# First experts of a PEER layer selected between the splits of the query projection, and ten row buffers for the first token tile

## The reference

```
h2 = rms_norm(x, norm2_g)
q = (h2 @ wq).reshape(T, 8, 2, 128)
scores = einsum('thcd,hcnd->thcn', q, keys)
s_top, i_top = top_k(scores, 16)
cand = s_top[:, :, 0, :, None] + s_top[:, :, 1, None, :]
cand_idx = i_top[:, :, 0, :, None] * 128 + i_top[:, :, 1, None, :]
best, pos = top_k(cand.reshape(T, 8, 256), 16)
idx = take_along_axis(cand_idx.reshape(T, 8, 256), pos, axis=-1)
gate = softmax(best)
hid = gelu(einsum('td,thkd->thk', h2, U[idx]))
x = x + einsum('thk,thkd->td', gate * hid, Vt[idx])
out = rms_norm(x, norm_f_g)
```

## Time and profile before

| | |
|---|---|
| median of 3 runs | 2193.09 us (2183.55 to 2193.47) |
| profiled execution | 2183.11 us, of which span 2181.4 us |
| busy: PE, DVE, ACT, POOL | 1477.1, 1641.9, 837.4, 975.7 us |
| splits (L798), 136 | 314.7 us, 2315 ns each |
| dots (L1331) read from `acc`, 189 | 428.3 us, 2284 ns each |
| gathers of U (L450), 256 | 250.5 us of GpSimd, 979 ns each |
| GpSimd products (L458), 63 | 285.6 us, 4533 ns each |

### The profile page before, as it was taken

One profiled execution on the slowest core, in us unless ns is written; L12 is line 12 of the kernel. 1 busy time (PEld: TensorE's weight loads), 2 busy tenths in 40 slices (PEclk: granted clock), 3 DMA queues, 4 the chain that ended last, 5 costly groups with the idle time before them and its releaser, 6 DMA issues.

```text
span 2181.4 us, 26401 instructions
## 1 busy us (share of the span) xinstructions
PE 1477.1 (68%) x9809; PEld 1368.3 (63%) x9809; DVE 1641.9 (75%) x2172; ACT 837.4 (38%) x1008; POOL 975.7 (45%) x692
## 2 busy tenths in 40 slices
PE   6999999999999999700000000113358999999996
PEld 6987998899999889700000000113247999899996
DVE  5465774545654555798898899998878999999997
ACT  4353433333433444112121221446666444444443
POOL 1002220000000000188888878877747776667763
PEclk9999999999999999855555555555569999999998
DMA  5555443434455554399999999999905999999996
GB/s 194 173 175 191 137 153 126 155 136 158 171 174 175 194 192 168 144 422 421 418 415 414 416 386 404 419 404 369 359 26 191 357 359 354 346 369 356 360 357 224
DMA packets 151526, 597.80 MB, mean 274 GB/s; under 512 B 14688, under 2 KB 14704, under 8 KB 118000
## 3 DMA queue, kind: packets, MB, share of 16 engines
q0 software_dynamic: 58048, 356.02, 41.3%
q1 hardware_dynamic: 93360, 240.22, 31.2%
HBM read 594.09 MB, written 2.10 MB: 273 GB/s over the span
## 4 chain that ended last, share of the span: by engine, by line
PE 47%; issue 15%; DVE 14%; DMA 11%; POOL 8%; ACT 4%; DVEq 0%; POOLq 0%; SPq 0%; ACTq 0%
PE acc L1470 9%; PE acc L1473 8%; PE acc L1472 8%; DMA slots<-in_peer_u,expert 8%; DVE slots L1331 7%; POOL starts L487 6%; DMA starts<-in_v_gather,expert 3%; PE acc L1487 3%; PE acc L1489 3%; PE acc L1488 3%; PE scr L1740 3%; POOL slots L450 1%; PE scr L1535 1%; PE acc L1770 1%; PE acc L1772 1%
## 5 line engine op out<-in xcount | busy, mean ns | idle before, releaser
L798 DVE TENSOR_TENSOR w_lo<-raw,w_hi 128x2048 fp32r<-128x2048 f32 x136 | 314.7, 2315 | 319.5 <-ACT w_hi L503 318.5
L1331 DVE SCALAR_TENSOR_TENSOR slots<-slots,acc 128x2048 f32<-128x2048 f32 x189 | 428.3, 2284 | 36.4 <-DMA slots<-in_peer_u,expert 34.6
L503 ACT ACTIVATE w_hi<-raw 128x2048 fp32r<-128x2048 f32 x136 | 260.1, 1913 | 435.6 <-PE acc L1473 308.0
L487 POOL DMA_INDIRECT starts<-in_v_gather,expert x256 | 344.5, 1346 | 155.4 <-DVE X L1411 103.8
L450 POOL DMA_INDIRECT slots<-in_peer_u,expert x256 | 250.5, 979 | 288.8 <-DVE expert L1267 188.4
L458 POOL TENSOR_TENSOR slots<-slots,N 128x2048 f32<-128x2048 f32 x63 | 285.6, 4533 | 31.6 <-DMA slots<-in_peer_u,expert 31.2
L1470 PE MATMUL acc<-hT_hi,w_hi 128*128 128x256 f32 x1024 | 294.6, 288 | 3.1 <-PE acc L1473 2.5
L1472 PE MATMUL acc<-hT_lo,w_hi 128*128 128x256 f32 x1024 | 292.2, 285 | 0.0
L1473 PE MATMUL acc<-hT_hi,w_lo 128*128 128x256 f32 x1024 | 292.1, 285 | 0.0
L1740 PE MATMUL scr<-hot_a,hot_b 128*128 128x128 f32 x512 | 101.4, 364 | 280.5 <-ACT hot_a L732 171.9
L771 ACT ACTIVATE v_hi<-v_raw 128x1408 fp32r<-128x1408 f32 x128 | 177.0, 1384 | 282.3 <-PE scr L1772 203.6
(11 more groups left out here) (262 smaller groups left out, 3324.1 us busy)
## 6 DMA issues: line engine op xcount, KB each, us to landing
raw<-in_w_in SPq DMA_DIRECT2D x88, 1024.0 KB, 4.8
v_raw<-in_v_dense SPq DMA_DIRECT2D x128, 704.0 KB, 6.4
raw<-in_w_o SPq DMA_DIRECT2D x16, 1024.0 KB, 5.1
raw<-in_peer_wq SPq DMA_DIRECT2D x16, 1024.0 KB, 5.0
raw<-in_w_a_up SPq DMA_DIRECT2D x8, 1024.0 KB, 5.1
raw<-in_w_b_up SPq DMA_DIRECT2D x8, 1024.0 KB, 5.0
slots<-in_peer_u,expert POOLq DMA_INDIRECT x256, 9.0
starts<-in_v_gather,expert POOLq DMA_INDIRECT x256, 6.6
```

Of the source, the lines that this page charges most:

```text
L487: pool.indirect_dma_start(starts[s % CRING][:, :], None, v_gather[:, :], bass.IndirectOffsetOnAxis(ap=expert[:, s // NSEL, s % NSEL:s % NS ...
L503: a.activation(w_hi[:, m % 2, :, :], raw[:, m % 2, :, :], ACT.Copy).then_inc(hi_ready, 1)
L798: v.tensor_tensor(w_lo[:, m % 2, :, :], raw[:, m % 2, :, :], w_hi[:, m % 2, :, :].bitcast(fp32), ALU.subtract).then_inc(lo_ready, 1)
L1331: v.scalar_tensor_tensor(out=slots[:, j, :], in0=slots[:, j, :], scalar=1.0, in1=row, op0=ALU.mult, op1=ALU.mult, accum_out=hid[:, t, k:k + 1]
```

## The change

`slots` becomes ten buffers, placed one by one (`ROW_AT`, in KB): the first two at 24 and 152 KB, where the projection has nothing, then the eight of before. Rows 0 to 3 use buffers 0 to 3, which all lie outside the projection's buffers; so do rows 4 to 7, after rows 0 to 3 are used. From row 4 to row 123 the ten go round, from row 124 on the last eight. Gather 0 now waits for `group_done` = `G_WQ` and gather 8, in place of gather 2, for `G_END`. On VectorE all eight parts of pair 0 and the dots of rows 0 to 3 stand between the splits of groups 1 to 3; row 3 is a VectorE row now, so there are 62 GpSimd products. Score 0 stands behind the first unit of group 1 on PE instead of the second. The sums move from `hid` to the room of `fox_mask`, since `hid` shares its room with `h2T_hi`, which the projection still reads.

```diff
+ROW_AT = (24, 152, 32, 40, 48, 56, 64, 72, 80, 88)
+LAST_TEN = 124
...
 def on_pool(q):
-    return q % FOUR == FOUR - 1 and q != GATHERS - 1
+    return q % FOUR == FOUR - 1 and FOUR <= q < GATHERS - 1
+
+def buffer_of(q):
+    if q < FOUR:
+        return q
+    if q < LAST_TEN:
+        return (q - FOUR) % len(ROW_AT)
+    return 2 + (q - LAST_TEN) % SLOTS
...
-        slots = at("slots", 32, [SLOTS, D])
+        slots = [at(f"slots{j}", kib, [D]) for j, kib in enumerate(ROW_AT)]
...
+        hid_sum = fox_mask[:, :].rearrange("p (t k) -> p t k", t=NT)
...
-                if q == 2:
+                if q == 0:
+                    pool.wait_ge(group_done, G_WQ)
+                if q == 2 * FOUR:
                     pool.wait_ge(group_done, G_END)
-                if q >= SLOTS:
-                    pool.wait_ge(row_used[j], q // SLOTS)
+                if uses_before(q, j):
+                    pool.wait_ge(row_used[j], uses_before(q, j))
...
-                if n:
+                if on_pool(FOUR * n - 1):
                     product(FOUR * n - 1)
...
-            for n in range(1, 4):
-                lo(G_WQ + n, 0)
-                lo(G_WQ + n, 1)
-                copy_q(n - 1)
-                lo(G_WQ + n, 2)
-                copy_scores(n - 1)
-                if n < 3:
-                    top_keys(0, 2 * n - 2)
-                lo(G_WQ + n, 3)
-                if n < 3:
-                    top_keys(0, 2 * n - 1)
-                else:
-                    for part in range(4, 8):
-                        select_part(0, 0, part)
+            lo(G_WQ + 1, 0)
+            copy_q(0)
+            lo(G_WQ + 1, 1)
+            copy_scores(0)
+            select_part(0, 0, 0)
+            lo(G_WQ + 1, 2)
+            select_part(0, 0, 1)
+            select_part(0, 0, 2)
+            lo(G_WQ + 1, 3)
+            select_part(0, 0, 3)
+            select_part(0, 0, 4)
+            lo(G_WQ + 2, 0)
+            select_part(0, 0, 5)
+            lo(G_WQ + 2, 1)
+            copy_q(1)
+            select_part(0, 0, 6)
+            lo(G_WQ + 2, 2)
+            select_part(0, 0, 7)
+            copy_scores(1)
+            lo(G_WQ + 2, 3)
+            dve.wait_ge(h2_ready, NT)
+            lo(G_WQ + 3, 0)
+            dot(0)
+            lo(G_WQ + 3, 1)
+            copy_q(2)
+            dot(1)
+            lo(G_WQ + 3, 2)
+            copy_scores(2)
+            dot(2)
+            lo(G_WQ + 3, 3)
+            dot(3)
             copy_q(3)
...
-                    if not on_pool(q):
+                    if q >= FOUR and not on_pool(q):
                         dot(q)
...
-                    if n and m == 1:
+                    if n and m == (n > 1):
                         score(n - 1)
```

More of the change, by code:

```diff
@@ L97, in on_pool, with uses_before @@
 def on_pool(q):
-    return q % FOUR == FOUR - 1 and q != GATHERS - 1
+    return q % FOUR == FOUR - 1 and FOUR <= q < GATHERS - 1
[5 more added lines that the diff above has]
+    return 2 + (q - LAST_TEN) % SLOTS
+def uses_before(q, j):
+    return sum(buffer_of(p) == j for p in range(q))
 def spread(g):
@@ L304, in build @@
         granted, granted_w = sem("granted"), sem("granted_w")
-        row_landed = [sem(f"row_landed{j}") for j in range(SLOTS)]
-        row_used = [sem(f"row_used{j}") for j in range(SLOTS)]
+        row_landed = [sem(f"row_landed{j}") for j in range(len(ROW_AT))]
+        row_used = [sem(f"row_used{j}") for j in range(len(ROW_AT))]
         h2_rows, product_ready = sem("h2_rows"), sem("product_ready")
@@ L694, in sum_product @@
             def sum_product(q):
-                act.wait_ge(product_ready, q // FOUR + 1)
-                row = slots[:, q % SLOTS, :]
-                a.activation(row, row, ACT.Copy, accum_out=hid[:, q // NSEL, q % NSEL:q % NSEL + 1]
-                             ).then_inc(row_used[q % SLOTS], 1)
+                act.wait_ge(product_ready, sum(map(on_pool, range(q + 1))))
+                row = slots[buffer_of(q)][:, :]
+                a.activation(row, row, ACT.Copy, accum_out=hid_sum[:, q // NSEL, q % NSEL:q % NSEL + 1]
+                             ).then_inc(row_used[buffer_of(q)], 1)
             def weight_curves(t):
@@ L737, in _ @@
                     rows_to_psum(1)
-                if i < GROUPS - 1:
+                if on_pool(FOUR * i + FOUR - 1):
                     sum_product(FOUR * i + FOUR - 1)
@@ L1285, in copy_scores, with dot @@
                 dve.sem_inc(scr_free[half], 1)
[L1287 to L1300 removed]
+            def dot(q):
+                t, k, j = q // NSEL, q % NSEL, buffer_of(q)
+                row = N1[:, t, :]
+                if q >= FOUR and k >= 2:
+                    dve.wait_ge(h2_rows, 2 * t + 2)
+                    row = acc[:, :, :].rearrange("p a n -> p (a n)")
+                dve.wait_ge(row_landed[j], 16 * (uses_before(q, j) + 1))
+                v.scalar_tensor_tensor(out=slots[j][:, :], in0=slots[j][:, :], scalar=1.0, in1=row,
+                                       op0=ALU.mult, op1=ALU.mult, accum_out=hid_sum[:, t, k:k + 1]
+                                       ).then_inc(row_used[j], 1)
+            lo(G_WQ + 1, 0)
[29 more added lines that the diff above has]
+            dot(3)
             copy_q(3)
@@ L1321, in hot_first @@
                                 ALU.is_equal).then_inc(a_ready[2], 1)
-            def dot(q):
-                t, k, j = q // NSEL, q % NSEL, q % SLOTS
-                row = N1[:, t, :]
-                if k >= 2:
-                    dve.wait_ge(h2_rows, 2 * t + 2)
-                    row = acc[:, :, :].rearrange("p a n -> p (a n)")
-                dve.wait_ge(row_landed[j], 16 * (q // SLOTS + 1))
-                v.scalar_tensor_tensor(out=slots[:, j, :], in0=slots[:, j, :], scalar=1.0, in1=row,
-                                       op0=ALU.mult, op1=ALU.mult, accum_out=hid[:, t, k:k + 1]
-                                       ).then_inc(row_used[j], 1)
             def weights(t):
-                for j in range(SLOTS):
-                    dve.wait_ge(row_used[j], (t + 1) * NSEL // SLOTS)
+                for j in range(len(ROW_AT)):
+                    dve.wait_ge(row_used[j], uses_before((t + 1) * NSEL, j))
                 g3 = gate[:, :].rearrange("p (h k) -> p h k", h=H)
```

23 lines of the change are left out of this document (11 added, 12 removed).

## The result

| us | before | after |
|---|---|---|
| median | 2192.07 (6 runs, 2183.55 to 2194.54) | 2172.43 (6 runs, 2163.77 to 2174.65) |
| profiled execution, its span | 2183.11, 2181.4 | 2163.77, 2162.1 |
| projection's last product begins | 909.10 | 913.81 |
| first gather; first gather behind the projection | 913.67, the same one | 874.65 (row 0); 914.99 (row 8) |
| gather of row 36 | 1002.50 | 984.54 |

The ratio is 0.9917 (95%: 0.99 to 0.9934), 0.83% faster. The forecast was 2172.0 us. The profiled executions lie at the low end of the runs on both sides and are 19.3 us apart.

What follows compares the result with a forecast made beforehand. The row stream (DMA) was taken as the limit from 920 to 1240 us, with later work following the rows. 19.9 + 2.6 - 0.9 = 21.6 us off the median 2193.09 gave 2171.5, predicted as 2172; range 2159 to 2175, whole range up to 2184.

Steps and rivals of the forecast that it cites:

- The rows that leave the stream: Gathers 0 to 7 move into the projection; eight rows of 2.485 us each gain 19.9 us.
- the hold of 0.9: After the seam, gathers wait for VectorE to free buffers; gather 16 lands 0.9 us late, once; bounds 0 to 3 us.
- The seam: From projection to row stream: gather 8 begins at 911.1 instead of 913.67, a gain of 2.6 us.
- the raw loads: Projection's loads beside the four early gathers: no delay to PE, taken as 0, at most some 5 us.
- (a): Group 1, unit 2 of the projection: the split ends 0.3 us after PE could have begun.
- (b): Group 2, unit 0 of the projection: parts 3 and 4 delay the next split, PE begins 0.9 us late.
- (c): Group 3, unit 3 of the projection: scores 2 and dot 2 come first, PE begins 0.8 us late.
- the two old waits: PE's two waits for late splits in the kernel before, 0.3 us each, were to go, saving 0.6 us.
- the second rival: A raw load waits behind the four early gathers, PE stalls 5 us or more; gain 16, 2177 us; chance 0.07.
- The rival that VectorE sets the pace: Behind the seam only VectorE's 9.4 us lead counts, 2184 us; chance 0.13, shared with the lead lost after 1240 us.
- PE's clock: Rival: a new wait in the projection halves PE's clock for eight units, costing 46 us; 2217 us, chance 0.05.
- It does what it says: Rival it doesn't: rows 4 to 7 are held, only four rows leave the stream; 2181 us, chance 0.05.

Runs made afterwards that it cites:

- Four rows early: Changed kernel with gather 4 instead of gather 8 waiting for the projection's end, so four rows leave the stream; 2182.13 us, ratio 0.996.
- none early: Changed kernel with all gathers and dots 0 to 3 behind the projection, early selection and ten buffers kept; 2186.54 us, ratio 0.9991.
- order: Changed kernel with VectorE's splits and selection parts in the projection reordered so that no split comes late; 2173.26 us, ratio 0.9924.
- both: Changed kernel with VectorE's reordered splits and selection and the early gathers queued one at a time; 2166.37 us, ratio 0.9891.
- after again: The changed kernel, unaltered, measured and traced a second time; 2173.65 us, ratio 0.9918.
- Paced: Changed kernel with gathers 1, 2 and 3 each waiting for one more split of group 3; 2168.79 us, ratio 0.9896.
- work added at row 64: Changed kernel with three unused VectorE maxima, 5.3 us in all, before the dots of group i = 16; 2168.78 us, ratio 0.9905.
- eight buffers: Changed kernel with a ring of eight buffers instead of ten from row 8 on; 2182.53 us, ratio 0.9966.
- work added at the seam: Changed kernel with three unused VectorE maxima, 5.3 us in all, behind the last copy_q; 2176.28 us, ratio 0.9943.
- held product: Changed kernel with GpSimd's product of row 139 waiting until the weights of tile 0 are ready; 2170.89 us, ratio 0.9909.
- both and held: Changed kernel with VectorE's reordering, the paced early gathers and the wait before the product of row 139 together; 2164.17 us, ratio 0.988.

## Why the prediction was right, and where it was off

The time (2172.0 predicted, 2172.43 measured) and the main mechanism are right. One term was taken at nothing and was not, and the total hides it. That the total lies within 0.5 us is partly luck: the gain was put at 21.6 us and the medians give 19.6, but the kernel before came out 1.0 us lower than the median the forecast started from, and the forecast was rounded up by 0.5.

- **The rows that leave the stream: right.** 19.9 less the hold of 0.9 is 19.0; the traces give 19.28 from the seam to row 36, and the hold shows as 0.8 us of lead between rows 12 and 16. Four rows early instead of eight cost 9.0 us of it in the trace, and none early gave the kernel before.
- **The seam: wrong by 3.9 us.** Predicted +2.6, measured -1.3. The mis-sized term is that of the raw loads: "I take 0". The load of group 3, unit 1, landed in 11.3 us, not 5.0, and PE waited 2.17 us for it; the load behind it took 13.0 us, which the prediction did not price. By the starts the two cost 2.6 us: unit 1 came 8.17 us behind unit 0 where a unit takes 5.79 (885.82 to 893.99), and unit 2 came 7.73 behind unit 1 where a unit with scores takes 7.49. The range given for the term, 0 to 5 us, held that. Over the traces with four gathers in a row the longest wait was 1.4 to 5.2 us. The rest: the profiled execution was already 0.97 us later when the changed part began (group 1 at 834.04 instead of 833.07), and gather 8 came 0.9 us behind PE's last product (914.09 to 914.99), not 0.3. That 0.3 was the idle time of PE at a new group, while the gather came 0.9 us behind PE's last product in order, both and after again too. The waits of the order came about as placed, counted as in the prediction, by starts: (a) 0.2 for 0.3, (b) 0.8 for 0.9 (1.07 less the 0.30 that each group's start has), (c) 0.6 for 0.8, and the two old waits that go are 0.2 each, not 0.3. That is 0.3 less than counted, and 0.97 + 2.6 + 0.6 - 0.3 = 3.9.
- **The price of the load, shown.** Paced gathers bring the landing back to 5.1 to 6.9 us and take the wait away; a better order without pacing only moves the wait to the next load (5.1 us). This was the second rival as a mechanism. It had a chance of 7% as an outcome of 2177 us; the wait was nearer 2 than 5 us and is inside what the median can't tell from the forecast.
- **The Trainium skill's rule on turns did not carry the number I took from it.** I had read "DMA: Bandwidth & Descriptors", section on SWDGE, HWDGE and iDMA, as about twice the load's own time; the runs show 11.3 and 13.0 us in after, 14.4 with four rows early and 15.8 in order, so two to three times. The page's section on queues, rings and completion order has the turns by packet, a bundle of descriptors. If both queues gave as many pieces a turn, a load of 2 KB pieces would get one byte for four of a row of 8 KB pieces, and five times the 2.5 us of 1 MB is an estimate of 12.4 us. That is near the 11.3 to 13.4 us of most traces and not near order's 15.8; no run here changed the size of the pieces, so it is an inference and not shown.
- **VectorE and the buffers: right.** Dot 4 stands at 924.12 where 921.4 was predicted, 2.7 us late, because the projection ended late: from there VectorE took 9.9 us to it (`copy_q` begins at 914.22), where 10.4 were counted. Waits for rows 18.0 us (17 predicted), none in the first 85 us. The rival that VectorE sets the pace is refuted by the work added at row 64, for the stretch up to 1240 us. No work was added in the later stretch, where VectorE is 96% busy (129.71 of 135 us from 1320 us on); there it can only be said that the lead of after does not shrink (18.0 us at row 36, 18.3 at row 160, 17.4 at the end). The same work at the seam, and eight buffers, show that the slack begins only when the stream is caught up.
- **PE's clock: refuted as an outcome, but there is something in it.** In after's own trace the granted clock is 1.00 through (b), through the 2.17 us and up to 914 us. In other traces it did fall behind the wait for the load: waits of 1.4 and 1.6 us (work added at the seam, held product) and 2.17 us left it at 1.00 over 884 to 914 us; 3.2, 3.9 and 5.1 us (after again, eight buffers, order) brought it to 0.94, 4.3 and 5.2 us (work added at row 64, four rows early) to 0.89. The mean gives 1.8 and 3.3 us lost, which is too much where the clock fell before the wait was over; by the starts of the units it is 1.5 to 1.6 us in the first three and 2.6 to 2.7 in the last two (10.1 us from unit 1 to unit 2 instead of 7.49). Then the clock was full again; my 46 us assumed eight units at half. So the true price of a late load is its wait and up to 2.7 us more, which the prediction's bound of 5 us left out.
- **It does what it says.** Rows 4 to 7 are early: with four rows only, 9.4 us are missing.
- **The profiled and the median gain.** 18.0 us of lead at row 36 and 17.4 at row 255 leave 1.9 of the profiled 19.3 us behind the last gather (2181.4 - 1576.22 = 605.2 us before, 603.25 after). The change has nothing there, and I leave it open as a difference between executions.

What stays open: why executions of one kernel differ by 6 to 17.5 us where nothing is held. The traces show three parts, the start of the projection (832.59 to 836.27 us over the kernels), the loads with the clock behind them, and short VectorE instructions that meet a product. The held product removes the one at the weights, and its runs lay closer (2.9 us against 12.9), but four and six runs don't show that the spread is due to it.

## What to carry to other kernels

Work that is bound by DMA later can be put under a stage that leaves DMA half idle, and its worth is the number of transfers that leave the stream times their pitch. That holds only if buffers keep the lead until the consumer has caught up, which the lead row by row shows. Queue such transfers one at a time between the loads that the stage itself needs: a load with 2 us of slack doesn't survive four 1 MB gathers ahead of it, and PE pays for a long wait twice, in the wait and in the clock behind it.

## What the runs showed of the hardware

- A 1 MB load on SyncE's queue, 5.0 us alone, took 10 to 15.8 us as one of the two loads issued behind four gathers of 1 MB, in all eight traces but for one load of 7.7 (order), and 5.1 to 7.8 with the gathers one at a time (paced, both, both and held).
- A VectorE instruction of 0.18 to 0.29 us that meets a product of GpSimd lasts until that product ends, 4.1 to 5.1 us in the rows above, a cast with one input too. Whether they meet hung on 0.1 to 0.5 us of their starts, so the same code has it in one execution and not in another.
- A gather begun beside a split in the projection took 2.89 us to issue instead of 0.94 (875.99 us), without a GpSimd product near. In eight traces (after, four rows early, order, paced, both, held product, both and held, work added at the seam), each gather of the projection that began while a split or a dot from `N` was running took 2.0 to 2.9 us, and every other one 0.94 to 1.04.
- Inside the projection PE's clock fell to 1.2 GHz behind single waits of 3.2 us and more, for 3.6 to 6.6 us by the mean clock of 30 us (1.5 to 2.7 us lost by the starts of the units), and not behind 2.17 us. Before the last scores PE kept the full clock through a wait of 1.59 us and did the last 16 products in 2.02 us; after 4.76 us it was at half, 3.75 us.
